# Two conditions in one product, a turned final norm, a gather in parts, and roots read from the bank

## The reference

```python
mod = (silu_c @ ada_w[layer] + ada_b[layer])[:, None, :]        # latent tokens
mod_c = (silu_cc @ ada_w[layer] + ada_b[layer])[None, None, :]  # context tokens
sh1, sc1, g1, sh2, sc2, g2 = jnp.split(mod, 6, axis=-1)
h = _rmsnorm(x, norm_w[layer, 0]) * (1.0 + sc1) + sh1
```

```python
for e in range(N_EXPERTS):
    y_e = swiglu_ffn(t, w_gate_up[e], w_down[e])
    out = out + combine[:, e:e + 1] * y_e
...
x = x + g2 * y
return rms_norm(x, final_norm)
```

## Time and profile before

| | us |
|---|---|
| median of 3 runs | 2381.2 |
| their range | 2380.38 to 2384.44 |
| the profiled execution's own time | 2389.65 |
| its span, first to last instruction | 2387.9 |
| PE busy | 2286.1 |
| DVE, ACT, POOL busy | 1071.8, 427.4, 109.4 |

### The profile page before, as it was taken

One profiled execution on the slowest core, in us unless ns is written; L12 is line 12 of the kernel. 1 busy time (PEld: TensorE's weight loads), 2 busy tenths in 40 slices (PEclk: granted clock), 3 DMA queues, 4 the chain that ended last, 5 costly groups with the idle time before them and its releaser, 6 DMA issues.

```text
span 2387.9 us, 39196 instructions
## 1 busy us (share of the span) xinstructions
PE 2286.1 (96%) x16904; PEld 1659.3 (69%) x16904; DVE 1071.8 (45%) x2046; ACT 427.4 (18%) x1004; POOL 109.4 (5%) x103
## 2 busy tenths in 40 slices
PE   6999999999999999999999989999998989999997
PEld 5444454488885886688887578888775867676765
DVE  4586454488886437745413655440444420000001
ACT  2311251100000023610002041100331311011101
POOL 0210210000002300000000000000012000000000
PEclk9999999999999999999999999999998999999997
DMA  9334522155454242148873227885441358989892
GB/s 332 135 129 163 165 68 84 57 175 178 142 199 115 56 150 71 37 164 295 292 206 122 103 71 246 281 273 168 156 165 44 109 189 306 343 307 341 308 340 77
DMA packets 305674, 427.49 MB, mean 179 GB/s; under 512 B 11539, under 2 KB 166706, under 8 KB 305258
## 3 DMA queue, kind: packets, MB, share of 16 engines
q1 hardware_dynamic: 302964, 422.03, 52.0%
q10 hardware_dynamic: 2550, 3.11, 0.4%
HBM read 423.88 MB, written 1.13 MB: 178 GB/s over the span
## 4 chain that ended last, share of the span: by engine, by line
PE 90%; DVE 5%; ACT 2%; issue 1%; DMA 1%; SPq 1%; DVEq 0%; ACTq 0%
PE banks L617 76%; PE banks L861 3%; ACT mem L2738 1%; DVE mem L1745 1%; PE banks L626 1%; PE banks L1545 1%; PE banks L966 1%; DVE mem L1742 1%; DVE mem L1738 1%; PE banks L1001 1%; PE banks L1375 1%; DMA mem<-in_ada_w 1%; DVE mem L2299 1%; PE banks L1609 1%; PE banks L825 1%
## 5 line engine op out<-in xcount | busy, mean ns | idle before, releaser
L617 PE MATMUL banks<-mem 128*32 128x128 f32 (+4 forms) x12788 | 1852.6, 358 | 27.3 <-ACT mem L2738 13.7
L617 PEld LDWEIGHTS banks<-mem 128*32 128x32 f32 (+2 forms) x12788 | 1330.5, 149 | 526.5 <-issue 315.4
L1742 DVE SCALAR_TENSOR_TENSOR mem<-mem 128x512 f32<-128x512 f32 (+6 forms) x509 | 366.6, 746 | 14.1 <-ACT mem L2738 4.5
L2738 ACT ACTIVATE mem<-banks 128x256 f32<-128x256 f32 (+7 forms) x347 | 137.2, 421 | 1099.2 <-PE banks L617 799.7
L2738 ACT ACTIVATE mem<-mem 128x256 f32<-128x256 f32 (+8 forms) x434 | 187.2, 483 | 687.1 <-DVE mem L1742 518.3
L1745 DVE TENSOR_TENSOR mem<-mem,banks 128x256 f32<-128x256 f32 (+3 forms) x88 | 43.3, 492 | 580.1 <-ACT mem L2738 551.4
L1742 DVE SCALAR_TENSOR_TENSOR mem<-banks,mem 128x256 f32<-128x256 f32 (+7 forms) x258 | 133.6, 543 | 342.8 <-PE banks L617 227.5
L1745 DVE TENSOR_TENSOR mem<-mem 128x256 f32<-128x256 f32 (+12 forms) x285 | 163.4, 584 | 37.2 <-ACT mem L2738 20.5
L1745 DVE TENSOR_TENSOR mem<-banks,mem 128x256 f32<-128x256 f32 (+3 forms) x223 | 93.1, 420 | 128.4 <-PE banks L617 78.6
L626 PE MATMUL banks<-mem 128*128 128x128 f32 (+3 forms) x392 | 62.1, 300 | 27.5 <-DMA mem<-in_ctx 11.1
L626 PEld LDWEIGHTS banks<-mem 128*128 128x128 f32 (+3 forms) x392 | 47.7, 155 | 52.8 <-DVE mem L1738 20.8
(11 more groups left out here) (182 smaller groups left out, 863.3 us busy)
## 6 DMA issues: line engine op xcount, KB each, us to landing
mem<-in_ada_w SPq DMA_DIRECT2D x96, 1024.0 KB, 9.9
mem<-in_moe_w_gate_up SPq DMA_DIRECT2D x64, 1024.0 KB, 13.0
mem<-in_ffn_w_in SPq DMA_DIRECT2D x44, 1024.0 KB, 6.7
mem<-in_moe_w_down SPq DMA_DIRECT2D x48, 768.0 KB, 9.6
mem<-in_moe_w_gate_up SPq DMA_DIRECT2D x32, 768.0 KB, 12.7
mem<-in_ffn_w_out SPq DMA_DIRECT2D x32, 704.0 KB, 6.9
mem<-in_ffn_w_gate_up SPq DMA_DIRECT2D x22, 1024.0 KB, 6.5
mem<-in_ab_w_in SPq DMA_DIRECT2D x16, 1024.0 KB, 7.7
```

What stands on the lines that cost most here:

```text
L617: ins = nc.tensor.matmul(o, lhsT, rhs, start=start, stop=stop)
L1742: return V.scalar_tensor_tensor(out=o, in0=a, scalar=sc, in1=b, op0=op0, op1=op1)
L2738: ac = lambda o, i, f, **k: nc.scalar.activation(o, i, f, **k)
```

## The change

1. *Opening.* `ada()` takes both conditions as a stationary operand of two columns: 32 products a panel (64 rows) in place of 64, whose results lie on two partitions of each group of 32. DVE copies the 128x128 result to memory (`ada_copied`), PE turns it (`ada_turned`), DVE adds the bias into `mod` (`ada_biased`). PE's order becomes: product 0, turn 0, product 1, turn 1, `norm_sum`, product 2, product 3, turn 2, turn 3, `norm_spread`. Two small memsets are added at DVE's start.
2. *Norms.* ACT takes the root straight from the bank (scale 1/1024, bias 1e-6 from a column), then DVE the reciprocal. DVE's scaling step is gone. This holds for the eight norms that remain.
3. *Experts.* `gather` takes the pairs it is to make. At the end of experts 0 to 5 PE makes one pair ahead of `turn_acts(2)` and one behind `turn_picks`; two experts together make the four pairs. `pair_picks` moves from the odd experts to the even ones before. Experts 6 and 7 are as before.
4. *End.* PE turns xT itself, block by block as DVE finishes it; ACT squares the four banks and sums each row (`accum_out`), DVE multiplies the banks by the norm's weight, which SP has loaded spread over all partitions; then sum, root, reciprocal, and DVE and ACT scale one token tile each, in halves; SP stores four quarters. A root on one value is put on ACT ahead, so that the table is there. `norm_sum`, `norm_spread` and the old norm go.

```diff
@@ -442,6 +443,12 @@
 y_own = work(12480, 2, 3 * P)
+fin = work(0, 2, D)
+fin_square = work(3840, 4, T2)
+fin_weight = work(9600, D)
+fin_sums = small[:, 0:4]
+fin_rs = small[:, 4:6]
+fin_eps = small[:, 6:7]
 slots = work(13312, NE + 2, 2)
@@ -599,10 +606,13 @@
-    fin = work(0, 2, D)
-    sp.wait_ge(s["final_copied"], 4)
-    sp.dma_start(out.rearrange("a (t p) n -> p (a t) n", p=P), fin).then_inc(s["out_stored"], 16)
-    sp.wait_ge(s["out_stored"], 16)
+    sp.dma_start(fin_weight, A["final_norm_2"].flatten().rearrange("(a n) -> a n", a=1).to_broadcast([P, D])).then_inc(s["rows_loaded"], 16)
+    for half in range(2):
+        for i, signal in enumerate(("final_copied", "final_scaled")):
+            sp.wait_ge(s[signal], half + 1)
+            sp.dma_start(out[0, i * P:(i + 1) * P, half * T2:(half + 1) * T2], fin[:, i, half * T2:(half + 1) * T2])\
+                .then_inc(s["out_stored"], 16)
+    sp.wait_ge(s["out_stored"], 64)
@@ -655,18 +665,28 @@
-    def ada(cond):
+    def ada_bank():
+        n = c["ada"].next()
+        if n > 2:
+            pe.wait_ge(s["ada_taken"], n - 2)
+        return PS[4 + c["ada"].place(2)]
+    def ada():
         w = panel(8, 512)
-        n = c["ada"].next()
-        if c["ada"].i is not None or n > 2:
-            pe.wait_ge(s["ada_taken"], c["ada"].ahead(2))
-        bank = PS[4 + c["ada"].place(2)]
-        for j in range(2):
-            for k in range(8):
-                by = conds[:, cond + j, k:k + 1].to_broadcast([P, 32])
-                for a in range(4):
-                    last = mm(quarter(bank, j, a), by, columns(w[:, k, :], a), k == 0, k == 7)
+        bank = ada_bank()
+        for k in range(8):
+            for a in range(4):
+                last = mm(bank[32 * a:32 * a + 2, 0:P], conds[:, 0:2, k], w[:, k, a * P:(a + 1) * P],
+                          k == 0, k == 7)
         last.then_inc(s["ada_ready"], 1)
+    def ada_turned(i, copied):
+        bank = ada_bank()
+        pe.wait_ge(s["ada_taken"], copied)
+        turn(bank[:, 0:P], ada_own[:, i % 2 * P:(i % 2 + 1) * P]).then_inc(s["ada_ready"], 1)
@@ -700,7 +720,7 @@
-        await_("norm_rooted", "rooted")
+        await_("norm_inverted", "rooted")
         for i in range(width // P):
@@ -917,11 +937,15 @@
     pe.wait_ge(s["cond_ready"], 4)
-    for _ in range(3):
-        ada(0)
+    for i in range(2):
+        ada()
+        ada_turned(i, c["ada"].n)
+    norm_sum(T2)
+    for i in (2, 3):
+        ada()
+    for i in (2, 3):
+        ada_turned(i, c["ada"].n - 1)
     if stop >= 1:
-        norm_sum(T2)
-        ada(0)
         norm_spread(T2)
@@ -1534,10 +1558,9 @@
-        def gather():
-            await_("picks_ready", "picks")
-            for pair in range(4):
+        def gather(pairs):
+            for pair in pairs:
                 bank = moved_item()
@@ -1617,7 +1640,8 @@
         with pe.If(most <= CAP):
-            gathered = gather()
+            await_("picks_ready", "picks")
+            gathered = gather(range(4))
             turn_picks()
@@ -1644,17 +1668,23 @@
                         put_back(e - 1, done)
-                if e % 2 and e < NE - 1:
-                    gathered = gather()
+                more = e < NE - 2
+                if more:
+                    if e % 2 == 0:
+                        await_("picks_ready", "picks")
+                    gather((e % 2 * 2,))
                 turn_acts(2, c["gu"].n)
+                turned = c["moved"].n
                 if e < NE - 1:
                     turn_picks()
+                if more:
+                    gathered = gather((e % 2 * 2 + 1,))
                 for m in range(2):
...
                         if m == 0 and first == 0:
-                            pe.wait_ge(s["moved_taken"], c["moved"].n - (2 if e < NE - 1 else 1))
+                            pe.wait_ge(s["moved_taken"], turned)
                         for k in range(first, end):
@@ -1703,15 +1733,12 @@
-    norm_sum(L, added=False)
-    norm_spread(L)
-    await_("dve_for_pe", "dve")
-    for t in range(2):
-        for half in range(2):
-            n = 2 * t + half
-            for b in range(4):
-                last = turn(PS[n][:, b * P:(b + 1) * P], hT[:, half * 4 + b, t * P:(t + 1) * P])
-            last.then_inc(s["x_turned"], 1)
+    for k in range(8):
+        pe.wait_ge(s["out_taken"], c["out"].n - 7 + k)
+        for t in range(2):
+            last = turn(PS[2 * t + k // 4][:, k % 4 * P:(k % 4 + 1) * P], xT[:, k, t * P:(t + 1) * P])
+            if k % 4 == 3:
+                last.then_inc(s["x_turned"], 1)
@@ -1801,13 +1828,31 @@
-    def norm(par, which, weight, parts, final=False, between=()):
-        await_("sum_ready", "sum")
+    def ada_copied(i):
+        await_("ada_ready", "ada")
+        V.tensor_copy(ada_own[:, i % 2 * P:(i % 2 + 1) * P], PS[4 + c["ada"].place(2)][:, 0:P]).then_inc(s["ada_taken"], 1)
+    def ada_biased(i):
+        await_("ada_ready", "ada")
+        v = PS[4 + c["ada"].place(2)][:, 0:P].rearrange("p (a r) -> p a r", a=4)[:, :, 0:2]
+        tt(mod[:, 0, 4 * i:4 * i + 4, 0:2], v, col("ada_b", 4 * i, 4).unsqueeze(2).to_broadcast([P, 4, 2]), ALU.add)\
+            .then_inc(s["ada_taken"], 1)
+    def last_adas():
+        for i in (2, 3):
+            ada_copied(i)
+        for i in (2, 3):
+            ada_biased(i)
+    def norm(par, which, weight, parts, final=False, between=None):
+        await_("norm_rooted", "sum")
         tiles = 2 * parts
-        link(scale(rstd[:, 0:tiles], PS[3][:, 0:tiles], 1.0 / D, EPS))
-        V.reciprocal(rstd[:, 0:tiles], rstd[:, 0:tiles]).then_inc(s["norm_meaned"], 1)
-        for i in between:
-            ada(col("ada_b", 0, 48), 0, i)
+        V.reciprocal(rstd[:, 0:tiles], rstd[:, 0:tiles]).then_inc(s["norm_inverted"], 1)
+        if between:
+            between()
         dve.wait_ge(s["ada_taken"], c["ada"].n)
@@ -2044,6 +2089,8 @@
         dve.nop().then_inc(s["gu_taken"], 1)
+    V.memset(norm_eps, EPS)
+    V.memset(PS[4][:, 0:P], 0.0)
     for k in range(8):
@@ -2054,11 +2101,12 @@
     c["panels"].n = 4
-    ada(col("ada_b", 0, 48), 0, 0)
+    ada_copied(0)
+    ada_biased(0)
     for m in range(8):
         add_square(m, T2, hT)
-    for i in (1, 2):
-        ada(col("ada_b", 0, 48), 0, i)
+    ada_copied(1)
+    ada_biased(1)
     dve.wait_ge(s["rows_loaded"], NROW * 16)
@@ -2072,7 +2120,7 @@
     if stop >= 1:
-        norm(0, 0, col("norm_w", 0, 8), 2, between=(3,))
+        norm(0, 0, col("norm_w", 0, 8), 2, between=last_adas)
         bank = item()
@@ -2644,6 +2692,7 @@
         V.tensor_scalar(slot_of, slot_of, -1.0, None, ALU.add).then_inc(s["dve_for_pe"], 1)
+        V.memset(fin_eps, EPS)
         V.memset(slots, -1.0)
@@ -2691,8 +2740,8 @@
                     tt(tok[:, L:3 * P], e_silu[:, 1, 0:P], PS[1][:, P:L]).then_inc(s["gu_taken"], 1)
-                    if q == 0 and e % 2 and e < NE - 1:
-                        pair_picks(e + 1)
+                    if q == 0 and e % 2 == 0 and e < NE - 2:
+                        pair_picks(e + 2)
                     if q == 0 and e < NE - 1:
@@ -2723,13 +2772,19 @@
                         add_out(1, 1, 1, m)
-    dve.wait_ge(s["out_taken"], c["out"].n)
-    norm(0, 0, col("final_norm_2"), 1, final=True)
-    dve.wait_ge(s["scaled"], c["scaled"].n)
-    dve.nop().then_inc(s["dve_for_pe"], 1)
-    for n in range(4):
-        dve.wait_ge(s["x_turned"], 8 + n + 1)
-        V.tensor_copy(work(0, 2, D)[:, n // 2, (n % 2) * 512:(n % 2 + 1) * 512], PS[n][:, :]).then_inc(s["final_copied"], 1)
+    dve.wait_ge(s["rows_loaded"], (NROW + 2) * 16)
+    for half in range(2):
+        h = slice(half * T2, (half + 1) * T2)
+        for t in range(2):
+            await_("act_for_dve", "act")
+            tt(fin[:, t, h], PS[2 * t + half][:, :], fin_weight[:, h])
+    sums = fin_sums.rearrange("p (t h) -> p t h", t=2)
+    post(tt(fin_rs, sums[:, :, 0], sums[:, :, 1], ALU.add), "dve_for_act", "fa")
+    await_("act_for_dve", "act")
+    post(V.reciprocal(fin_rs, fin_rs), "dve_for_act", "fa")
+    for half in range(2):
+        v = fin[:, 0, half * T2:(half + 1) * T2]
+        scale(v, v, fin_rs[:, 0:1]).then_inc(s["final_copied"], 1)
@@ -2759,8 +2814,8 @@
-        await_("norm_meaned", "norms")
-        ac(rstd[:, 0:tiles], rstd[:, 0:tiles], ACT.Sqrt).then_inc(s["norm_rooted"], 1)
+        await_("sum_ready", "norms")
+        ac(rstd[:, 0:tiles], PS[3][:, 0:tiles], ACT.Sqrt, scale=1.0 / D, bias=norm_eps).then_inc(s["norm_rooted"], 1)
@@ -3209,9 +3264,9 @@
-        def gathered(j):
-            for pair in range(4):
+        def gathered(j, pairs):
+            for pair in pairs:
                 moved(h_own[j][:, pair * 2:pair * 2 + 2, :], 4 * CAP, 2)
@@ -3233,7 +3288,7 @@
         with act.If(most <= CAP):
-            gathered(0)
+            gathered(0, range(4))
             moved(back[:, 0, :, :].rearrange("p a n -> p (a n)"), T2)
@@ -3246,11 +3301,14 @@
                     silu(P)
```

(22 more changed lines are left out.)

5 lines of the change are left out of this document (3 added, 2 removed).

## The result

The median of four timed runs is 2367.49 us (2365.88 to 2368.44), against 2382.82 us (2380.38 to 2389.17) for four of the kernel before beside them: a ratio of 0.9928, with a 95% interval of 0.9911 to 0.9944. On the 2381.2 us that the prediction started from that is 2364.1. Forecast was 2363.1, between 2358 and 2370.

The account below looks back on a forecast made before the run. PE, busy 2286.1 of 2387.9 us, was taken as the bound. Opening -3.4, norms +0.3, experts -2.7 and end -12.3 gave -18.1, subtracted from 2381.2 for a median of 2363.1 us, range 2358 to 2370.

Parts of the forecast that it names:

- The sum: Whole kernel: -3.4 + 0.3 - 2.7 - 12.3 = -18.1 us, for a median of 2363.1 us.
- the 8.4: Whole kernel: the profiled execution lies 8.4 us above the timed median, taken as the same in both kernels.
- Opening, forecast -3.4: Kernel start: 64 rows a panel, path through the fourth panel, first projection at 43.5; -3.4 us, between -5.0 and -1.5.
- the 0.8 kept back for it: First projection after the opening: it may meet the low clock, costing 1.7 us, of which half was taken.
- Norms, forecast +0.3: Seven norms: four with a table load +0.22 us each, three without -0.2 each; +0.3, between -0.6 and +1.5.
- Experts, forecast -2.7: Ends of experts 0, 2 and 4: gather pairs around the turns cover waits, 3 x 0.9 us saved; other end -1.5.
- PE's work stays the same: Experts' gather: splitting it adds no PE work, one pair being 1.37 us of the whole gather's 5.47.
- The rival, that ACT's copy of the pair delays the turned activations: Experts: turned activations come late by as much as was saved; +2.7 us, median 2365.8, chance 0.06.
- End, forecast -12.3: Kernel end: turns, bank-wise squares and products, quartered stores shorten the tail to 14.5 us; -12.3, between -14.7 and -11.4.
- The first rival: Kernel end: PE has a second code stop within its turns; +2.3 us, median 2365.4, chance 0.14.
- products of two columns do not share the array: Opening: each row costs what one alone does, 7.1 us a panel; opening +4.8, median 2371.3, chance 0.03.
- The case of little change: Opening's order set by loads and the end by the store: total within 0.2%, chance 0.01.

Follow-up runs that it names:

- c_before: The kernel before with no edit, run again; median 2383.46 us, ratio 0.9997.
- c_after: The changed kernel with no edit, run again; median 2365.62 us, ratio 0.9921 against the kernel before.
- n_tail: The changed kernel with the sixteen turns of the end put inside both arms of the branch; median 2366.74 us, ratio 0.9930 against the kernel before.
- p_end: The kernel before with the end alone changed; median 2374.38 us, ratio 0.9966.
- p_end_pad: The kernel before with the end alone changed and 32 empty instructions at the start of PE's program; median 2371.84 us, ratio 0.9951.
- p_norms: The kernel before with only the norms changed, roots taken straight from the bank; median 2384.16 us, ratio 0.9999.
- p_experts: The kernel before with only the experts' gather made in parts; median 2382.72 us, ratio 0.9998.
- n_all: The changed kernel with two loads issued after the first norm, one gather run an expert and end turns inside the branch; median 2362.52 us, ratio 0.9903.

## Why the prediction was right, and where not

**The sum** of -18.1 met a measured ratio that is worth -17.2 and medians that differ by 15.3; the median was 4.4 above the forecast, 1.6 of it because the kernel before ran at 2382.82 that time. By the stretches the change is worth about -15.7. The savings of the opening and of the experts were each taken 1.5 too large and the cost of the norms 0.3 too small, the saving at the end 1.0 too small. So it came out well partly because errors of both signs met; that is luck. The prediction also took the profiled execution to lie 8.4 above the median in both kernels. After, it lay 0.95 above (2368.44 against 2367.49): the 8.4 belonged to one execution.

**Opening, forecast -3.4.** The first profiles give -3.0, by the way foretold: 64 rows a panel, in 1.93 to 3.60; the copies and turns hidden; the path through the fourth panel. Forecast was a projection at 43.5, measured 44.65 and 43.11. Two parts of the term were off. The projection kept the full clock, so the 0.8 kept back for it was not paid; against that the fourth panel landed at 38.45, not 37.66. And the baseline was a bad case: with an opening at full clock the kernel before starts its projection at 44.2 to 44.7; the mean over the profiles is -1.9, near the weak end of the term's range (-1.5). The prediction read one execution's 5.37 and 5.31 as the kernel's usual.

**Norms, forecast +0.3, found +0.6.** At 1031 the table load ends last and the spread starts 0.51 after the root's start (1031.73, 1032.24), which is the reciprocal behind the root as predicted. PE waits 0.26 more there, forecast 0.22. Near 440, where the table was there, the root starts 0.04 after the sum, and 0.13 is saved, forecast 0.2. The root itself took 0.26 in place of 0.20, in all seven norms 0.4 that the sum left out, and 0.3 is what the term lacks. The final root, on a value in memory with the same kind of bias, took 0.29. By the Trainium skill (ScalarE: Activation LUTs, What ACT_TABLE_LOAD costs) each pointer operand adds about 93 ns: the final root agrees (0.09 over 0.20), the roots from the bank show two thirds of it (0.06), though they also read another source, which no run separates. By that figure the term would have been +0.95, by the prediction's sum +0.3; the traces lie between. A total of this size is below what the timed runs tell.

**Experts, forecast -2.7, found -1.15.** This is the step that failed, in the sentence "PE's work stays the same". The three waits did go. But each separate run of the gather's products costs 0.2 more than its rows do, and there are four where there was one: 0.6 for every two experts, 1.8 for six. 2.7 less 1.8 is 0.9, near the 1.15 that the boundaries show. The prediction divided 5.47 by four; the earlier trace rows alone had no row of a shorter run to warn of it. The rival, that ACT's copy of the pair delays the turned activations, did not occur: PE has no idle time there.

**End, forecast -12.3, found -13.6 in the first profile and -13.1 between `c_before` and `c_after`.** The tail was to be 14.5 and was 13.2. The order of events is the one foretold: one stop of 2.66, turns at the lower clock level, squares and products bank by bank, sum, root, scales, four stores. Two terms were too dear: the turns took 3.01 and not 3.68, at a granted clock of 0.63 (below; 0.50 before, last of the earlier trace rows), and DVE did not stop for 2.76 at its own way out: in `n_tail` its products follow the additions at once (2356.26). The stores took as long as expected: 4.5 from the first issue (2362.16) to the end of the span, forecast 4.3.

```profile
2356.00:2359.20 3.20, 3.01 (x16) 2.61 (x16) 1.99 (x5) 1.53 (x5) 0.00 (x0) 0.63 0.03 5
```

**The first rival** (a second stop, 0.14) did not occur in the changed kernel and did in `p_end` and `p_end_pad`, at 2.45 and 2.56. The same tail has it in one program and not in another, and nothing that I read before the runs tells which. The Trainium skill (Runtime: NRT & Kernel Launch, Instruction fetch mechanics) says that a taken branch out of the loaded blocks stalls the engine; the runs agree in that the 2.66 stands behind the way out of the branch and disappears when the turns stay inside it (`n_tail`), and in the 16 KB packets that end 1.5 before PE goes on. Where a further stop falls, its rule of 256 instructions did not let me foretell; in the runs it went with the old opening. That products of two columns do not share the array is refuted by 1.93 for 64 rows, 30 ns each. The case of little change is excluded by the interval.

## What to carry to other kernels

A product with small stationary operands in several column groups can take a second condition as a second column at no cost to the row (30 ns here, 29 before), but what then ends last in an opening is a load: look which constants were issued ahead of the weights that the first products need, as deferring 960 KB and the router's weights brought the first projection forward by 2.9 us on average here, halving the products by 1.9. Splitting a run of equal products to cover waits cost 0.2 us for each piece, so cover a wait with the longest run that does it. A small step taken out of a chain helps only where nothing else ends last: the roots from the bank cost 0.6 us, because behind a table load the reciprocal was no longer hidden. And profile the kernel before twice: a stretch that the change doesn't touch and that differs by 5 us between two executions tells how much of a difference of spans is worth nothing.

## What the runs showed of the hardware that was not expected

A run of 128x192 products between products on parts of the array costs 0.1625 us a row and 0.2 once: 1.50 for 8 rows, 2.80 for 16, 5.40 for 32.

PE's second stop near the end of the program (2.1 to 2.8) is there in all six profiles with the old opening (before, `c_before`, `p_norms`, `p_experts`, `p_end`, `p_end_pad`) and in none of the six with the new one that could show it; 32 instructions more at the start of the program did not move it. A 16 KB packet of the `instruction` queue ends 1.35 to 1.55 us before PE goes on at all 18 stops.

The store of 1 MB landed 4.0 after its issue and quarters of it 2.5 (median): a fourth of the bytes takes more than half of the time.

SP's four issues of stores took 1.83 in the changed kernel, 2.92 in `n_tail` and 3.82 in `n_all`, with the same instructions; one issue alone was long, with a 16 KB `instruction` packet inside it.
